# The recurrent mixer computed in two halves of its heads

## The chip, the cores and the metric

One core of a Trainium2 chip runs a whole forward pass of four layers in one launch. The metric is device time in microseconds (us), the median of several executions. A profiled execution of the same program gives the trace. Its engines are PE (TensorE, the matrix products), ACT (ScalarE), DVE (VectorE), POOL (GpSimd) and SP, the queue that issues the loads of the weights.

## What is computed

512 tokens of width 1024, everything in float32. The first block has a gMLP and convolution mixer, experts, a recurrent mixer, and experts again. The second block has two layers of attention with a gated feed-forward. The change lies in the recurrent mixer alone, cut here from the reference:

```python
def mixer_rglru(h, w_in, conv_w, conv_b, w_a, b_a, w_x, b_x, lam, w_out):
    gate, xr = jnp.split(h @ w_in, [D_RNN], axis=-1)          # 1024 -> 2 x 1024
    gate = jax.nn.gelu(gate)
    xr = causal_conv(xr, conv_w) + conv_b                     # 4 taps along the tokens
    xh = xr.reshape(bsz, t_len, LRU_HEADS, LRU_HEAD_DIM)      # 8 heads of 128
    r = sigmoid(einsum('bthi,hij->bthj', xh, w_a).reshape(...) + b_a)
    i = sigmoid(einsum('bthi,hij->bthj', xh, w_x).reshape(...) + b_x)
    log_a = (8.0 * r) * log_sigmoid(lam)
    a = exp(log_a)
    b = sqrt(-expm1(2.0 * log_a)) * (i * xr)
    _, hseq = associative_scan(combine, (a, b), axis=1)       # along the tokens, each channel by itself
    return (gate * hseq) @ w_out
```

No channel of it depends on another between the products with `w_in` and `w_out`, except within a head of 128 channels. So the eight heads can be worked in any order.

## The kernel before

Each engine has one program, a Python closure in `mixer_rglru`: `tensor`, `scalar`, `vector`, `gpsimd`. An engine works its instructions in the order in which they are written, and waits on counting semaphores (`x_conv`, `i_x`, `a_sq`, `q_done`, `b_root`, `scanned`, `y_mult`, `yhi`, `ylo`). Order and buffers are both fixed by hand.

**The products.** A float32 matrix is split into a high part (rounded to fp32r, by ACT in `W.hi`) and a low remainder (by DVE for even halves, by POOL for odd ones, in `W.lo`), and a product is three fp32r matmuls per tile: high by high, high by low, low by high. One 1024 x 512 piece of `w_in` is two units of 1 MB, so four halves, which are the four steps of a product of 96 matmuls. A raw unit sits in one of 4 raw slots and a split half in one of 6 split slots. Half s+6 is split when PE has used half s. SP issues the loads in the order of the plan (`plan_lru`), each when its raw slot was left: by the two low splits of the unit before it or, for the unsplit unit `gates`, by PE's last matmul with it. A load that waits holds all the later ones.

**The order on PE.** `xr 0` and `xr 1` (the two 512-column halves of the recurrent branch, heads 0 to 3 and 4 to 7), `gt 0` (first half of the gate branch), the gates (16 float32 matmuls, two for each head, line 1026, each of which shows as two in the trace), `gt 1`, then the product with `w_out` in two halves, `lruo 0` (line 605) and `lruo 1` (line 625). Step k of `lruo` waits for `ylo` k, the low part of feature block k of gate times state.

**The other engines.** ACT copies the results of `xr` out of PSUM (`bank_to`, line 680) and DVE convolves them with four taps (lines 1094 and 1097) into XC. After `gt 0` with its gelu, ACT takes the 16 sigmoids (line 680 with a bias from PK), POOL multiplies i by the convolved input (line 1134), and ACT takes exp, square and tanh for each head (lines 1051, 1057, 1058), DVE one combination (line 1106, `q_done`), then ACT eight square roots (line 1061), and DVE for each head a product and the scan (lines 1114, 1115). POOL multiplies heads 0 to 3 by the gate (line 1139), ACT rounds them to the high part (line 1064), DVE takes the low part (line 1110). Those four low parts stand on DVE's queue behind the sixth scan. Heads 4 to 7 get their product, high and low part after `gt 1` (lines 1124, 1074, 1110).

The square of a head lies in XT, a buffer of four heads that also holds what the convolution reads; so the squares of heads 4 to 7 wait for the combination of the head four before. AA (the decays) lies over XC, so exp of a head waits until POOL has read its convolved input.

The PSUM banks are eight, taken in turn; a product of 4 banks waits until the bank's last user has been read out.

Of the kernel before, what the change touches and what calls it, by code (L numbers as in the profile page):

```python
# [11 lines left out]
ALU = mybir.AluOpType  # L12
# [91 lines left out]
def up(signal, instruction):  # L104
    instruction.then_inc(signal.h, 1)
    signal.n += 1
    return signal.n
# [195 lines left out]
def program(nc, A, pack, const, out):  # L303
# [690 lines left out]

    def plan_lru():
        w = A["c_w_in"][0]
        for key, c0 in ((("xr", 0), 1024), (("xr", 1), 1536), (("gt", 0), 0)):
            plan_cols(key, w, c0, 512)
        W.add("gates", [(8, 128, A["c_w_a"][0].rearrange("h i j -> i h j")),
                        (8, 128, A["c_w_x"][0].rearrange("h i j -> i h j"))], split=False)  # L1000
        plan_cols(("gt", 1), w, 512, 512)
        plan_out("lruo", A["c_w_out"][0])

    def mixer_rglru(rows, late):
# [5 lines left out]
        AA = at(8192, 8, 512)  # L1010
        YH = at(8192, 8, 512, dt=F32R)
        YL = at(20480, 8, 512, dt=F32R)
        gates = W.of["gates"][0]
        H = rows.H

        def tensor():
            tensor_first_product(rows, ("xr", 0), 4, 512, ba, True)
            for key in (("xr", 1), ("gt", 0)):
                tensor_product(key, ALL4, 512, H, ba, feature=True)
            PE.wait_dma(W.s_raw[gates.slot], gates.arrived)  # L1020
            wg = W.raw[gates.slot][:, :].rearrange("p (g h j) -> p g h j", g=2, h=8)
            for h in range(8):
                PE.wait_ge(x_conv, h + 1)
                for g in range(2):
                    bank = banks.take(ba)
                    n = up(ba.full, pe.matmul(bank[:, :], wg[:, g, h, :], XC[:, h, :], start=True, stop=True))
            W.raw_consumed_at[gates.n] = (ba.full, n)
            tensor_product(("gt", 1), ALL4, 512, H, ba, feature=True)
            tensor_out("lruo", (lambda k: YH[:, k, :], lambda k: YL[:, k, :]), lambda k: PE.wait_ge(ylo, k),
                       ahead=lambda: tensor_experts_turn(1, 0))  # L1030

        def scalar():
            scalar_rows(rows, None, late, False)
            scalar_log_sigmoid(SM[:, 40:48])
            for s in range(2):
                def taps_in(s=s):
                    for o in range(4):
                        bank = ba.next(S)
                        if s:
                            S.wait_ge(x_conv, o + 1)  # L1040
                        bank_to(XT[:, o, :], bank[:, :])
                scalar_product(("xr", s), taps_in)
            scalar_product(("gt", 0), scalar_banks(lambda o: GT[0][:, o, :], func=ACT.Gelu_apprx_tanh))
            for h in range(8):
                for dst, bias in ((RB, "c_b_a"), (IB, "c_b_x")):
                    bank = ba.next(S)
                    bank_to(dst[:, h, :], bank[:, :], ACT.Sigmoid, bias=col(bias, h))
            S.wait_ge(lam_ready, 1)
            for h in range(8):
                S.wait_ge(i_x, h + 1)  # L1050
                up(a_exp, act.activation(AA[:, h, :], RB[:, h, :], ACT.Exp, scale=SM[:, 32 + h:33 + h]))
                S.wait_ge(a_exp, h + 1)
                if h < 4:
                    S.wait_ge(x_conv, 4 + h + 1)
                else:
                    S.wait_ge(q_done, h - 3)
                up(ss, act.activation(XT[:, h % 4, :], AA[:, h, :], ACT.Square))
                up(a_sq, act.activation(RB[:, h, :], RB[:, h, :], ACT.Tanh, scale=SM[:, 80 + h:81 + h]))
            for h in range(8):
                S.wait_ge(q_done, h + 1)  # L1060
                up(b_root, act.activation(RB[:, h, :], RB[:, h, :], ACT.Sqrt))
            for m in range(4):
                S.wait_ge(y_mult, m + 1)
                up(yhi, act.activation(YH[:, m, :], GT[0][:, m, :], ACT.Copy))

            def gelu_1():
                for o in range(4):
                    bank = ba.next(S)
                    S.wait_ge(q_done, 5 + o)
                    bank_to(GT[1][:, o, :], bank[:, :], ACT.Gelu_apprx_tanh)  # L1070
            scalar_product(("gt", 1), gelu_1)
            for m in range(4, 8):
                S.wait_ge(y_mult, m + 1)
                up(yhi, act.activation(YH[:, m, :], GT[1][:, m - 4, :], ACT.Copy))
            scalar_product(("lruo", 0))
            S.wait_ge(y_mult, 8)
            S.wait_ge(ylo, 8)
            load_moe(1)
            sqrt_table()
            return scalar_last_product(("lruo", 1), TAIL, lambda: scalar_experts_turn(1, 0))  # L1080

        def vector():
            vector_rows(rows, None, late, False)
            log_sigmoid_in(cols("c_lambda", 0, 8), SM[:, 40:48])
            log_sigmoid(SM[:, 32:40], cols("c_lambda", 0, 8), SM[:, 40:48], SM[:, 48:56], SM[:, 56:64])
            vstep(dve.tensor_scalar(SM[:, 32:40], SM[:, 32:40], 8.0, None, ALU.mult))
            up(lam_ready, dve.tensor_scalar(SM[:, 80:88], SM[:, 32:40], -1.0, None, ALU.mult))
            for s in range(2):
                def taps(s=s):
                    for o in range(4):  # L1090
                        m = 4 * s + o
                        y, g = XC[:, m, :], XT[:, o, :]
                        V.wait_ge(ba.free, m + 1)
                        vstep(dve.tensor_scalar(y, g, col("c_conv_w", 24 + m), col("c_conv_b", m), ALU.mult, ALU.add))
                        for j in (2, 1, 0):
                            d = 3 - j
                            ins = dve.scalar_tensor_tensor(y[:, d:T], g[:, 0:T - d], col("c_conv_w", 8 * j + m),
                                                           y[:, d:T], ALU.mult, ALU.add)
                            if j:
                                vstep(ins)  # L1100
                        up(x_conv, ins)
                vector_product(("xr", s), taps)
            vector_product(("gt", 0))
            for h in range(8):
                V.wait_ge(a_sq, h + 1)
                up(q_done, dve.scalar_tensor_tensor(RB[:, h, :], XT[:, h % 4, :], 1.0, RB[:, h, :], ALU.add, ALU.mult))

            def low(m):
                V.wait_ge(yhi, m + 1)
                up(ylo, dve.tensor_tensor(YL[:, m, :], GT[m // 4][:, m % 4, :], f32(YH[:, m, :]), ALU.subtract))  # L1110
            for h in range(8):
                V.wait_ge(b_root, h + 1)
                V.wait_ge(i_x, h + 1)
                vstep(dve.tensor_tensor(IB[:, h, :], IB[:, h, :], RB[:, h, :], ALU.mult))
                up(scanned, dve.tensor_tensor_scan(RB[:, h, :], AA[:, h, :], IB[:, h, :], 0.0, ALU.mult, ALU.add))
                if h == 5:
                    for m in range(4):
                        low(m)
            vector_product(("gt", 1))
            for m in range(4, 8):  # L1120
                V.wait_ge(ba.free, 8 + 4 + 16 + m - 3)
                V.wait_ge(scanned, m + 1)
                y = GT[1][:, m - 4, :]
                V.wait_total(y_mult, up(y_mult, dve.tensor_tensor(y, y, RB[:, m, :], ALU.mult)))
                low(m)
            return vector_out("lruo", norm_for_experts(1), lambda: vector_experts_turn(1, 0))

        def gpsimd():
            gpsimd_late(late)
            for key in (("xr", 0), ("xr", 1), ("gt", 0)):  # L1130
                gpsimd_product(key)
            for h in range(8):
                G.wait_ge(ba.free, 8 + 4 + 2 * h + 2)
                up(i_x, pool.tensor_tensor(IB[:, h, :], IB[:, h, :], XC[:, h, :], ALU.mult))
            for m in range(4):
                G.wait_ge(ba.free, 8 + m + 1)
                G.wait_ge(scanned, m + 1)
                y = GT[0][:, m, :]
                up(y_mult, pool.tensor_tensor(y, y, RB[:, m, :], ALU.mult))
            for key in (("gt", 1), ("lruo", 0), ("lruo", 1)):  # L1140
                gpsimd_product(key)
# [1407 lines left out]
```

## Time and profile before

| | us |
|---|---|
| median of 3 runs | 2706.59 |
| lowest and highest | 2702.04, 2707.36 |
| the profiled execution | 2703.67 |
| its span in the profile | 2702.3 |
| PE busy in it | 2592.2 |
| the recurrent mixer's products, first to last start | about 700 to 869 |

Times in a trace are counted from the start of the span. A timeline line shows when a group of like instructions began, its length, engine, line, operation and count, and in brackets how long the engine had been idle before it and what released it ("issue": nothing that the profile shows). Starts of two neighbouring groups give PE's pace best, since the ends of matmuls are modelled.

### The profile page before, as it was taken

What the parts mean: (1) busy time and instruction counts of PE and PEld (TensorE: products, weight loads), DVE (VectorE), ACT (ScalarE), POOL (GpSimd) and SP (SyncE); (2) the same over time, 40 slices, a digit from 0 to 9 for tenths busy, and PEclk for the clock granted to TensorE, in tenths of its full rate; (3) what the DMA queues carried; (4) which work ended last, traced back from release to release, by engine and by line L of the source; (5) the groups of instructions that cost most, each with busy time, mean ns of one, the idle gap of its engine ahead of it and who ended that gap; (6) DMA issues with size and microseconds to landing.
All of it is one profiled execution on the core that took longest, in us unless ns stands there. A gap on an engine that the chain in (4) does not pass through costs nothing.

```text
span 2702.3 us, 33251 instructions
## 1 busy us (share of the span) xinstructions
PE 2592.2 (96%) x13432; PEld 1818.3 (67%) x13432; DVE 1148.7 (43%) x2169; ACT 899.4 (33%) x1740; POOL 360.3 (13%) x165
## 2 busy tenths in 40 slices
PE   7998999999998899999979999999999999999999
PEld 6875444444766444444467778888888777888887
DVE  2543323332646332232256343562554534365254
ACT  3431111111464111111154554442345445443233
POOL 3200000000331000000021011222222001122222
PEclk9999999999898999999989999999999999999999
DMA  5229999999311999999932011223231201223212
GB/s 198 79 81 418 419 422 421 421 421 418 118 62 57 419 419 421 421 421 420 421 122 79 32 63 48 94 94 110 68 113 59 79 33 62 79 94 109 78 63 86
DMA packets 139003, 543.28 MB, mean 201 GB/s; under 512 B 18784, under 2 KB 30304, under 8 KB 89696
## 3 DMA queue, kind: packets, MB, share of 16 engines
q1 hardware_dynamic: 129232, 536.94, 50.8%
q10 hardware_dynamic: 9616, 4.18, 0.6%
q8 instruction: 109, 1.79, 0.3%
q14 instruction: 46, 0.38, 0.0%
HBM read 538.99 MB, written 2.10 MB: 200 GB/s over the span
## 4 chain that ended last, share of the span: by engine, by line
PE 90%; DVE 5%; ACT 2%; issue 2%; DMA 0%; POOL 0%; SPq 0%; DVEq 0%; ACTq 0%
PE ps L603 23%; PE ps L1363 16%; PE ps L605 14%; PE ps L1385 8%; PE ps L1338 5%; PE ps L625 4%; PE ps L537 4%; PE ps L1398 3%; PE ps L1939 2%; PE ps L1399 2%; PE ps L1912 2%; PE ps L1931 1%; PE ps L538 1%; PE ps L455 1%; DVE w L278 1%
## 5 line engine op out<-in xcount | busy, mean ns | idle before, releaser
L603 PE MATMUL ps<-w,w 128*128 128x512 f32 x2976 | 679.9, 390 | 2.6 <-POOL w L278 2.6
L603 PEld LDWEIGHTS ps<-w,w 128*128 128x128 f32 x2976 | 559.0, 188 | 119.7 <-POOL w L278 3.4
L278 POOL TENSOR_TENSOR w<-w,w 128x1024 fp32r<-128x1024 f32 (+2 forms) x139 | 337.2, 2435 | 2182.9 <-ACT w L270 2182.9
L1363 PE MATMUL ps<-w,w 128*64 128x512 f32 x2048 | 451.6, 594 | 1.8 <-issue 1.8
L605 PE MATMUL ps<-w,w 128*128 128x512 f32 (+1 forms) x1872 | 410.9, 381 | 18.2 <-issue 15.2
L270 ACT ACTIVATE w<-w 128x1024 fp32r<-128x1024 f32 (+2 forms) x260 | 252.7, 1001 | 436.2 <-PE ps L603 196.9
L605 PEld LDWEIGHTS ps<-w,w 128*128 128x128 f32 x1872 | 339.9, 189 | 85.5 <-issue 19.7
L278 DVE TENSOR_TENSOR w<-w,w 128x1024 fp32r<-128x1024 f32 (+2 forms) x121 | 200.7, 1666 | 386.8 <-ACT w L270 384.4
L1363 PEld LDWEIGHTS ps<-w,w 128*64 128x64 f32 x2048 | 146.0, 137 | 285.6 <-issue 285.6
L1615 DVE TENSOR_TENSOR X<-ps,X 128x512 f32<-128x512 f32 x256 | 163.0, 682 | 163.0 <-PE ps L1399 161.9
L1385 PE MATMUL ps<-w,w 128*64 128x512 f32 x1024 | 226.8, 595 | 0.8 <-ACT w L1449 0.8
L1385 PEld LDWEIGHTS ps<-w,w 128*64 128x64 f32 x1024 | 70.6, 137 | 139.8 <-issue 138.9
L2345 DVE SCALAR_TENSOR_TENSOR w<-ps,PK,w 128x511 f32<-128x511 f32 (+1 forms) x176 | 131.8, 749 | 75.8 <-ACT w L2301 72.6
L1338 PE MATMUL ps<-w,w 128*128 128x256 f32 x1024 | 131.3, 288 | 4.9 <-DVE w L1586 4.9
L1338 PEld LDWEIGHTS ps<-w,w 128*128 128x128 f32 x1024 | 130.2, 196 | 7.6 <-DVE w L1586 5.1
L1603 DVE TENSOR_TENSOR w<-ps,w 128x512 f32<-128x512 f32 x32 | 34.8, 1086 | 212.1 <-PE ps L1363 212.1
L625 PE MATMUL ps<-w,w 128*128 128x512 f32 x528 | 122.1, 390 | 0.9 <-DVE X L703 0.9
L1398 PE MATMUL ps<-w,w 128*128 128x512 f32 x256 | 111.8, 437 | 4.6 <-DVE w L1622 4.6
L625 PEld LDWEIGHTS ps<-w,w 128*128 128x128 f32 x528 | 98.7, 188 | 21.5 <-issue 1.3
L1622 DVE SCALAR_TENSOR_TENSOR w<-ps,w,w 128x512 fp32r<-128x512 f32 x64 | 45.1, 747 | 159.1 <-ACT w L1494 159.1
L1494 ACT ACTIVATE w<-ps,w 128x512 fp32r<-128x512 f32 x64 | 40.5, 684 | 204.0 <-PE ps L1385 204.0
L537 PE MATMUL ps<-w,w 128*128 128x256 f32 x768 | 99.9, 294 | 8.3 <-POOL w L278 6.7
(251 smaller groups left out, 2325.3 us busy)
## 6 DMA issues: line engine op xcount, KB each, us to landing
w<-in_moe_w_gate SPq DMA_DIRECT2D x128, 1024.0 KB, 14.0
w<-in_moe_w_up SPq DMA_DIRECT2D x128, 1024.0 KB, 16.4
w<-in_moe_w_down SPq DMA_DIRECT2D x128, 1024.0 KB, 13.0
w<-in_w_up SPq DMA_DIRECT2D x40, 1024.0 KB, 5.1
w<-in_w_down SPq DMA_DIRECT2D x20, 1024.0 KB, 5.1
w<-in_w_in SPq DMA_DIRECT2D x16, 1024.0 KB, 5.1
w<-in_ab_w_in SPq DMA_DIRECT2D x10, 1024.0 KB, 5.1
w<-in_c_w_in SPq DMA_DIRECT2D x8, 1024.0 KB, 5.1
```

What stands on the lines that cost most here:

```text
L270: up(self.whi, self.S.e.activation(hi, raw, ACT.Copy))
L278: up(self.wlo[self.low[s][0]], lane.e.tensor_tensor(lo, raw, hi.bitcast(F32), ALU.subtract))
L537: return pe.matmul(bs[o][:, t], w[:, P * o:P * o + P], a(k)[:, t], start=first, stop=stop)
L603: ins = pe.matmul(bank[:, :], wp[:, k, P * o:P * o + P], ap(k0 + k), start=first, stop=stop)
L605: ins = pe.matmul(bank[:, 0:width], ap(k0 + k)[:, P * o:P * o + P], wp[:, k, :], start=first, stop=stop)
L625: ins = pe.matmul(bank_of(o)[:, 0:width], ap(k)[:, P * o:P * o + P], wp, start=(k == 0 and pi == 0), stop=(hi is rows[-1][0] and pi == 2))
L1338: i = pe.matmul(bank[:, 256 * k:256 * k + 256], HB[part][:, c, t:t + P], SELR[:, c, :], start=(part == 0 and c == 0), stop=(part == 1 and ...
L1363: ins = pe.matmul(bank[64 * e:64 * e + 64, :], XG[p % 3][:, 4 * u + k, 64 * e:64 * e + 64], w[e][:, k, :], start=(u == 0 and k == 0), stop ...
L1385: ins = pe.matmul(two[n][64 * e:64 * e + 64, :], HDT[:, 2 * u + k, 64 * e:64 * e + 64], w[e][:, k, 512 * n:512 * n + 512], start=(u == 0 a ...
L1398: pe.matmul(bank[:, :], s_, YH[:, 512 * n:512 * n + 512], start=True, stop=False)
L1615: up(bx.free, dve.tensor_tensor(x, bank[:, :], x, ALU.add))
L2345: ins = dve.scalar_tensor_tensor(y[:, d:T], bank[:, 0:T - d], col("conv_w_2", 132 * i + 44 * tap + f), y[:, d:T], ALU.mult, ALU.add)
```

## The change

The heads are worked in two groups, 0 to 3 and 4 to 7, and every engine's program follows. PE's order becomes `xr 0`, `xr 1`, gates of heads 0 to 3, `gt 0`, gates of heads 4 to 7, `gt 1`, `lruo`. The gates' weights become two unsplit units. ACT's chain (sigmoids, exp, square, tanh, then roots) runs once for each group; the squares of heads 0 to 3 go to the buffer of `gt 0`. The roots and scans of the first group are put into the work for `gt 0`, behind its first split. The splits of the first two halves of `gt 1`, which stood in the work for `xr 1`, are put behind the first group's chain (`behind_gates`). The low parts of heads 0 to 3 follow all the scans.

```diff
     def plan_lru():
         w = A["c_w_in"][0]
-        for key, c0 in ((("xr", 0), 1024), (("xr", 1), 1536), (("gt", 0), 0)):
-            plan_cols(key, w, c0, 512)
-        W.add("gates", [(8, 128, A["c_w_a"][0].rearrange("h i j -> i h j")),
-                        (8, 128, A["c_w_x"][0].rearrange("h i j -> i h j"))], split=False)
-        plan_cols(("gt", 1), w, 512, 512)
+        for s in range(2):
+            plan_cols(("xr", s), w, 1024 + 512 * s, 512)
+        for s in range(2):
+            W.add("gates", [(4, 128, A[name][0][4 * s:4 * s + 4].rearrange("h i j -> i h j")) for name in ("c_w_a", "c_w_x")],
+                  split=False)
+            plan_cols(("gt", s), w, 512 * s, 512)
...
+        HEADS = (range(0, 4), range(4, 8))
+        behind_gates = late_halves(("xr", 1), 2)
+        def squared(h):
+            return GT[0][:, h, :] if h < 4 else XT[:, h - 4, :]
         def tensor():
...
+            tensor_product(("xr", 1), ALL4, 512, H, ba, feature=True)
+            for s in range(2):
+                gates = W.of["gates"][s]
+                wg = W.need_raw(gates, PE)[:, 0:1024].rearrange("p (g h j) -> p g h j", g=2, h=4)
+                for h in HEADS[s]:
+                    PE.wait_ge(x_conv, h + 1)
+                    for g in range(2):
+                        bank = banks.take(ba)
+                        n = up(ba.full, pe.matmul(bank[:, :], wg[:, g, h % 4, :], XC[:, h, :], start=True, stop=True))
+                W.raw_consumed_at[gates.n] = (ba.full, n)
+                tensor_product(("gt", s), ALL4, 512, H, ba, feature=True)
...
         def scalar():
...
-                scalar_product(("xr", s), taps_in)
+                scalar_product(("xr", s), taps_in, tail=2 * s)
+            def decays(hs):
+                for h in hs:
+                    for dst, bias in ((RB, "c_b_a"), (IB, "c_b_x")):
+                        bank = ba.next(S)
+                        bank_to(dst[:, h, :], bank[:, :], ACT.Sigmoid, bias=col(bias, h))
+                S.wait_ge(lam_ready, 1)
+                for h in hs:
+                    S.wait_ge(i_x, h + 1)
+                    up(a_exp, act.activation(AA[:, h, :], RB[:, h, :], ACT.Exp, scale=SM[:, 32 + h:33 + h]))
+                    S.wait_ge(a_exp, h + 1)
+                    if h > 3:
+                        S.wait_ge(x_conv, h + 1)
+                    up(ss, act.activation(squared(h), AA[:, h, :], ACT.Square))
+                    up(a_sq, act.activation(RB[:, h, :], RB[:, h, :], ACT.Tanh, scale=SM[:, 80 + h:81 + h]))
+            def roots(hs):
+                for h in hs:
+                    S.wait_ge(q_done, h + 1)
+                    up(b_root, act.activation(RB[:, h, :], RB[:, h, :], ACT.Sqrt))
+            def gelu_0():
+                for o in range(4):
                     bank = ba.next(S)
+                    S.wait_ge(q_done, 1 + o)
+                    bank_to(GT[0][:, o, :], bank[:, :], ACT.Gelu_apprx_tanh)
+            decays(HEADS[0])
+            for h in behind_gates:
+                W.hi(h)
+            scalar_product(("gt", 0), gelu_0, second=lambda: roots(HEADS[0]))
+            decays(HEADS[1])
+            roots(HEADS[1])
...
         def vector():
...
+                vector_product(("xr", s), taps, tail=2 * s)
...
-                if h == 5:
-                    for m in range(4):
-                        low(m)
+            factors(HEADS[0])
+            for h in behind_gates:
+                W.lo(h, V)
+            vector_product(("gt", 0), second=lambda: scans(HEADS[0]))
+            factors(HEADS[1])
+            scans(HEADS[1])
+            for m in range(4):
+                low(m)
             vector_product(("gt", 1))
...
         def gpsimd():
             gpsimd_late(late)
+            for s in range(2):
+                gpsimd_product(("xr", s), tail=2 * s)
+            def inputs(hs):
+                for h in hs:
+                    G.wait_ge(ba.free, 8 + 4 * (h // 4) + 2 * h + 2)
+                    up(i_x, pool.tensor_tensor(IB[:, h, :], IB[:, h, :], XC[:, h, :], ALU.mult))
+            inputs(HEADS[0])
+            for h in behind_gates:
+                W.lo(h, G)
+            gpsimd_product(("gt", 0))
+            inputs(HEADS[1])
             for m in range(4):
-                G.wait_ge(ba.free, 8 + m + 1)
+                G.wait_ge(ba.free, 8 + 8 + m + 1)
                 G.wait_ge(scanned, m + 1)
```

`factors` is the combination of line 1106 for a group of heads, and `scans` the product and scan of lines 1114 and 1115.

## Rows read from the trace of the kernel before

**Rows 1.** The page: engines' busy time and share of the span.
```profile
PE 2592.2 (96%) x13432; PEld 1818.3 (67%) x13432; DVE 1148.7 (43%) x2169; ACT 899.4 (33%) x1740; POOL 360.3 (13%) x165
```

**Rows 2.** PE's waits over the span: total, times, longest.
```profile
PE ps L605 <- issue: 15.2, 1, 15.2
```

**Rows 3.** PE's timeline, from xr 1 to lruo 1.
```profile
726.63 43.71 PE L603 MATMUL ps<-w,w 128*128 128x512 f32 x192
770.18 13.89 PE L1026 MATMUL ps<-w,w 128*128 128x512 f32 x32
783.51 22.34 PE L603 MATMUL ps<-w,w 128*128 128x512 f32 x96
821.04 24.87 PE L605 MATMUL ps<-w,w 128*128 128x512 f32 x96 [15.19 <-issue]
845.75 4.47 PE L625 MATMUL ps<-w,w 128*128 128x512 f32 x19
```

**Rows 4.** Windows: length; busy PE, PEld, DVE, ACT, POOL; granted clock; DMA.
```profile
820.00:825.00 5.00, 3.96 (x9) 3.14 (x10) 4.97 (x6) 3.13 (x6) 2.17 (x2) 0.50 0.01 3
```

**Rows 5.** ACT's timeline, from gt 0's read-out to the splits before lruo.
```profile
768.33 2.64 ACT L680 ACTIVATE w<-ps 128x512 f32<-128x512 f32 x4 [0.98 <-PE ps L603]
773.23 5.56 ACT L680 ACTIVATE w<-ps,PK 128x512 f32<-128x512 f32 x9
...
784.81 1.28 ACT L1051 ACT_TABLE_LOAD   x1
786.11 0.72 ACT L1051 ACTIVATE w<-w,SM 128x512 f32<-128x512 f32 x1
...
793.69 0.71 ACT L1051 ACTIVATE w<-w,SM 128x512 f32<-128x512 f32 x1
...
801.36 1.28 ACT L1061 ACT_TABLE_LOAD   x1
802.66 4.28 ACT L1061 ACTIVATE w<-w 128x512 f32<-128x512 f32 x8
...
815.89 2.93 ACT L270 ACTIVATE w<-w 128x1024 fp32r<-128x1024 f32 x3
```

**Rows 6.** DVE's timeline: end of the convolution, first scans, low parts, heads 4 to 7.
```profile
760.47 1.22 DVE L278 TENSOR_TENSOR w<-w,w 128x1024 fp32r<-128x1024 f32 x1
...
803.32 0.69 DVE L1114 TENSOR_TENSOR w<-w,w 128x512 f32<-128x512 f32 x1 [1.25 <-ACT w L1061]
...
805.19 0.67 DVE L1114 TENSOR_TENSOR w<-w,w 128x512 f32<-128x512 f32 x1
...
818.17 4.57 DVE L1110 TENSOR_TENSOR w<-w,w 128x512 fp32r<-128x512 f32 x4
...
830.68 0.69 DVE L1124 TENSOR_TENSOR w<-w,w 128x512 f32<-128x512 f32 x1
...
832.74 0.69 DVE L1124 TENSOR_TENSOR w<-w,w 128x512 f32<-128x512 f32 x1
```

**Rows 7.** Line 1110 by itself: duration in ns, least, median, most.
```profile
L1110 DVE TENSOR_TENSOR w<-w,w x8: 677/692/2767, 818.2 to 838.3; 128x512 fp32r<-128x512 f32 x8
```

**Rows 8.** POOL's timeline: inputs of four heads, and the split beside line 1110.
```profile
774.57 4.94 POOL L1134 TENSOR_TENSOR w<-w,w 128x512 f32<-128x512 f32 x4 [0.23 <-ACT w L680]
...
817.96 2.43 POOL L278 TENSOR_TENSOR w<-w,w 128x1024 fp32r<-128x1024 f32 x1 [2.63 <-ACT w L270]
```

**Rows 9.** PE's timeline elsewhere: a short idle time and what ran after it.
```profile
1977.79 8.50 PE L603 MATMUL ps<-w,w 128*128 128x512 f32 x36 [1.28 <-POOL w L278]
```

**Rows 10.** SP's waits from 600 to 900 us.
```profile
SPq L254 <- PE ps L625: 83.9, 1, 83.9
```

**Rows 11.** SP's timeline: the first load for the experts of the second layer.
```profile
869.47 2.06 SPq L254 DMA_DIRECT2D w<-in_moe_w_gate  x4
```

**Rows 12.** DMA issues by source from 650 to 870 us: count, size, us to landing.
```profile
w<-in_c_w_in SPq DMA_DIRECT2D x8, 1024.0 KB, 5.1
```

More of the change, by code:

```diff
@@ L1012, in mixer_rglru @@
         YL = at(20480, 8, 512, dt=F32R)
-        gates = W.of["gates"][0]
         H = rows.H
+        HEADS = (range(0, 4), range(4, 8))
+        behind_gates = late_halves(("xr", 1), 2)
+        def squared(h):
+            return GT[0][:, h, :] if h < 4 else XT[:, h - 4, :]
         def tensor():
             tensor_first_product(rows, ("xr", 0), 4, 512, ba, True)
[L1018 to L1028, printed above, removed]
+            tensor_product(("xr", 1), ALL4, 512, H, ba, feature=True)
[9 more added lines that the diff above has]
+                tensor_product(("gt", s), ALL4, 512, H, ba, feature=True)
             tensor_out("lruo", (lambda k: YH[:, k, :], lambda k: YL[:, k, :]), lambda k: PE.wait_ge(ylo, k),
@@ L1041, in taps_in @@
                         bank_to(XT[:, o, :], bank[:, :])
-                scalar_product(("xr", s), taps_in)
-            scalar_product(("gt", 0), scalar_banks(lambda o: GT[0][:, o, :], func=ACT.Gelu_apprx_tanh))
-            for h in range(8):
-                for dst, bias in ((RB, "c_b_a"), (IB, "c_b_x")):
-                    bank = ba.next(S)
[L1047 to L1058, printed above, removed]
@@ L1059, in scalar @@
-            for h in range(8):
-                S.wait_ge(q_done, h + 1)
-                up(b_root, act.activation(RB[:, h, :], RB[:, h, :], ACT.Sqrt))
+                scalar_product(("xr", s), taps_in, tail=2 * s)
[13 more added lines that the diff above has]
+                    up(a_sq, act.activation(RB[:, h, :], RB[:, h, :], ACT.Tanh, scale=SM[:, 80 + h:81 + h]))
@@ L1101, in taps, with factors, scans @@
                         up(x_conv, ins)
[L1102 to L1106, printed above, removed]
+                vector_product(("xr", s), taps, tail=2 * s)
+            def factors(hs):
+                for h in hs:
+                    V.wait_ge(a_sq, h + 1)
+                    up(q_done, dve.scalar_tensor_tensor(RB[:, h, :], squared(h), 1.0, RB[:, h, :], ALU.add, ALU.mult))
+            def scans(hs):
+                for h in hs:
+                    V.wait_ge(b_root, h + 1)
+                    V.wait_ge(i_x, h + 1)
+                    vstep(dve.tensor_tensor(IB[:, h, :], IB[:, h, :], RB[:, h, :], ALU.mult))
+                    up(scanned, dve.tensor_tensor_scan(RB[:, h, :], AA[:, h, :], IB[:, h, :], 0.0, ALU.mult, ALU.add))
             def low(m):
@@ L1110, in low @@
                 up(ylo, dve.tensor_tensor(YL[:, m, :], GT[m // 4][:, m % 4, :], f32(YH[:, m, :]), ALU.subtract))
[L1111 to L1115, printed above, removed]
-                if h == 5:
-                    for m in range(4):
-                        low(m)
+            factors(HEADS[0])
[6 more added lines that the diff above has]
+                low(m)
             vector_product(("gt", 1))
@@ L1129, in gpsimd @@
             gpsimd_late(late)
[L1130 to L1134, printed above, removed]
+            for s in range(2):
+                gpsimd_product(("xr", s), tail=2 * s)
+            def inputs(hs):
+                for h in hs:
+                    G.wait_ge(ba.free, 8 + 4 * (h // 4) + 2 * h + 2)
[5 more added lines that the diff above has]
+            inputs(HEADS[1])
             for m in range(4):
-                G.wait_ge(ba.free, 8 + m + 1)
+                G.wait_ge(ba.free, 8 + 8 + m + 1)
                 G.wait_ge(scanned, m + 1)
```

## The prediction

> **What bounds the kernel now.** I read the page first: PE is busy 96% of the span [rows 1]. So only two things can shorten this kernel, less work on PE or less idle time of PE, and the change leaves PE's work as it is. The list of PE's waits comes next: one wait of 15.2 us stands before line 605, the first product with `w_out` [rows 2]. PE's timeline shows where it lies. `gt 1` starts at 783.51 and `lruo 0` only at 821.04 [rows 3]. A product of 96 matmuls takes 21.78 us from start to start: xr 1 and gt 0 are 192 matmuls and take 770.18 - 726.63 = 43.55 [rows 3]. So PE was through with `gt 1` at 783.51 + 21.78 = 805.3. `lruo 0` then takes 845.75 - 821.04 = 24.71, which is 2.93 more than 21.78, and the granted clock after the idle time is 0.50, the lower of the two levels, 1.2 GHz of 2.4 [rows 4]. In all the hole costs 821.04 - 805.29 + 2.93 = 18.7 us. That is the most the change can give, since the rest of the program is not touched.
>
> What fills the hole: `lruo 0` waits for the low part of head 0 (line 1110). It lies at the end of one chain through all eight heads, sigmoids, then exp, square and tanh (786.11 on), then roots (802.66 on) [rows 5], then scans (803.32 on), and then line 1110 at 818.17 behind the sixth scan [rows 6]. Its first instruction took 2.77 us where the median is 0.69 [rows 7], because POOL was splitting from 817.96 for 2.43 us beside it [rows 8]: it ended at 820.94, and PE went on at 821.04.
>
> **The change, part by part.** PE's work is the same in another order. The gates take 783.51 - 770.18 = 13.33 us [rows 3], now twice 6.67. If nothing waits, `gt 1` starts at 783.5 as before, and the second gates, call their start G, at 776.84. The first gates start at 748.40, `gt 0` at 755.07. I follow the chain from G, with distances of before.
>
> The second group's chain:
> - The first sigmoid came 3.05 us after the first matmul of the gates (773.23 - 770.18), behind gelu, a split and a table load, which stand there again. Nine took 5.56, so eight take 4.94: G + 8.0. This also fits the pace of PE (sigmoids were through 1.3 after the gates, at 784.8, and 6.67 + 1.3 = 8.0) [rows 3, 5].
> - Table load: exp starts 1.30 after the last sigmoid [rows 5]: G + 9.3.
> - Four heads of exp, square and tanh: the fifth exp started at 793.69, 7.58 after the first [rows 5], and the last tanh runs some 0.1 on: G + 17.0.
> - Table load before the roots 1.30, first product 803.32 - 802.66 = 0.66 after the first root [rows 5, 6]: G + 18.95.
> - Four products with scans, undisturbed 805.19 - 803.32 = 1.87 each [rows 6]: G + 26.4.
> - Line 1110 for head 0: 0.69 alone, 2.77 beside a split of POOL [rows 7]: G + 27.1 or G + 29.2.
>
> PE asks for it at G + 6.67 + 21.78 = G + 28.45. So it waits between nothing and 0.8 us. I take the disturbed value: four roots (half of 4.28), four rounded parts of about 0.55 and two splits of 0.98 (three took 2.93) [rows 5] put POOL's split at about G + 18.3 + 2.1 + 2.2 + 2.0 = G + 24.7, in the last scan, and it must come before line 1110 or in the middle of the scans. The scans themselves used to lose about 1 us each to POOL's products of line 1139; those products now come long before.
>
> The first group's chain lies beside `gt 0`. ACT: sigmoids through at 748.40 + 8.0 = 756.4 at the latest (PE's pace gives 756.0), exp from 757.3, tanh to 765.0, the two postponed splits and one more of 0.98 to 768.0, table load to 769.3, four roots to 771.5, two splits to 773.5, table load to 774.8. It must then read out `gt 0`, whose first bank is full 1.85 before the end of the product (770.18 - 768.33 [rows 3, 5]), at 775.0. So the 21.8 us of `gt 0` hide it with only 0.2 us to spare. That is the thin place: what ACT loses here goes straight into G's chain, less some 0.6 us that a late read-out gets back by running at 0.52 instead of at PE's pace. I add 0.3 us. DVE: the convolution ended at 760.47, and four inputs of POOL, 4.94 us in all [rows 8], can at most stand in its way for their own length, so 765.4; the roots need the combinations only from 769.3. DVE's next work for PE is the combination for G's group, so the first scans have some 15 us to spare. POOL has those 4.94 us and three splits of 2.43 [rows 8] in 25 us.
>
> Three table loads more, 1.3 us each, are all in these sums: the first group's sigmoid, exp and root loads lie beside `gt 0`. Costs of DVE's and POOL's moved instructions are nothing as long as PE has work; without `gt 0` over them the first group would cost some 19 us.
>
> The loads. SP now holds the two units of `gt 1` and the first of `w_out` until the first gates are done, 755.1; a load of 1 MB lands 5.1 later [rows 12], 760.2, and ACT splits it at 765. The other three units of `w_out` wait for the second gates, 783.5, as they now wait for the gates; no split asks before 800. The gates' weights are two loads of half the size, the first ahead of `gt 0`, with over 30 us to spare. Nothing here costs.
>
> Behind the first part: heads 4 to 7. DVE has three more low parts and two splits, up to about G + 35.5 with one disturbance (2.4), and then 2.06 us for each head (832.74 - 830.68 [rows 6]): the low part of head 4 at about 814.7. PE asks for it four steps of 2.72 us after its start at 806, at 817. Margin 2.3, and growing by 0.66 with each head. No second wait.
>
> What is late next: the first low part again, by 0.8 + 0.3 = 1.1 us, 1.2 with the 0.1 from the semaphore to PE's start (820.94 to 821.04). Such an idle time does not lower the clock: elsewhere, after 1.28 us, 36 matmuls took 8.50 [rows 9], that is 0.24 each, against 21.78 / 96 = 0.23 here. If it did, it would cost up to the 2.9 us of now.
>
> **The sum.** 18.7 - 1.2 = 17.5 us. Against the profiled execution's 2703.67 that is 2686.2; against the median 2706.59 it is 2689.1. The three timed runs and the profiled one have a mean of 2704.9, which gives 2687.4. I forecast 2688.
>
> Does the gain reach the end? The loads of the next experts start at 869.47 [rows 11], released by the last matmul of `lruo 1`, for which SP had waited 83.9 us [rows 10]. They move with PE, and so does all behind them.
>
> **The rivals.**
> (a) ACT overruns `gt 0`. For it: 0.2 us of margin in a row of 26 us; exp waits for POOL's product and the root for DVE's combination, and both engines have more beside them in the new order than in the rows I took. Against: all durations are measured. An overrun of 3 to 4 us makes PE wait 4 to 5 us in all, and with that the clock falls as now (2.9): 18.7 - 4.5 - 2.9 = 11.3 us, so 2694 from the forecast's base.
> (b) A change of function costs ACT more than the load. In the rows it doesn't: exp starts at 786.11, 1.30 after the load began, the roots 1.30 after theirs [rows 5]. If each change cost 1.4 us more, four in the first group would overrun `gt 0` by 5.3 and three behind G would add 4.1: 18.7 - 1.2 - 9.4 - 2.9 = 5.2 us of gain, 2700. The Trainium skill's page "ScalarE: Activation LUTs", section "What ACT_TABLE_LOAD costs", says just this (1283 ns and a drain of about 1380 ns), and its section on table sets advises to batch calls by set, which this change undoes. The trace has the 1.28 us and no drain behind it.
> (c) Slower: the four-head chain waits for the convolution of heads 4 to 7. DVE works it (760.47 before) ahead of the first combinations, and the roots, the read-out of `gt 0` and so PE's second gates now stand behind those. From about 769 on, each us of delay is a us of PE's time. To be slower by 0.2% the convolution would have to end after 793. POOL's four small products cannot do that by themselves; it takes DVE and POOL blocking each other far longer than the 2.1 us of one meeting (2.77 less 0.69) [rows 7].
> (d) The gain is taken back behind the mixer, because the experts' stage has a pace of its own: about 2705. Against it stand the two rows of the loads [rows 10, 11].
>
> **Chances.** Forecast (PE waits up to 3 us) 0.77, (a) 0.13, (b) 0.03, (c) 0.03, (d) 0.04. The lowest of the runs less the whole hole is 2702.0 - 18.7 = 2683.3, and I take 2682.5 as the low end; the high end takes in (a): 2697. About 0.2% or 5.4 us is what a measurement of this kernel can tell from no change. Faster 0.93, same 0.04, slower 0.03.
>
> **What would show it.** In the profile after: no wait of 15 us before `lruo 0`, but one of 0 to 2 us, with the granted clock at 1.00 through `lruo 0`; two groups of 16 gate matmuls, the second starting 28.4 us after the first; line 1110's first low part 27 to 30 us after the second gates' start; ACT's read-out of `gt 0` within 0.5 us of PE's last steps of it; four sets of roots and exp loads where there were two. Wrong would be: a wait of PE at the second gates (case a or b), drains behind the table loads (b), the first combination after 769 (c), or an experts' stage longer than before (d).

## The result, and the profile after

The changed kernel takes 2688.18 us (median of 4 runs, 2686.67 to 2689.76) against 2706.07 (4 runs, 2702.04 to 2707.36): ratio 0.9936, 95% interval 0.9919 to 0.9954. A second measurement of both gave 0.9941 (0.9927 to 0.9954), 2689.88 against 2706.4. By the medians that is 16.5 to 17.9 us less; the two intervals allow 12 to 22 us and 12 to 20 us. The forecast was 2688, its sum 17.5 us. So the time shows the gain, and its exact size is read from the traces.

PE's timeline of the changed kernel, the stretch of [rows 3] (start, length, engine, line, operation, count, idle time before):

```profile
726.00 21.95 PE L603 MATMUL ps<-w,w 128*128 128x512 f32 x96
747.79 7.03 PE L1032 MATMUL ps<-w,w 128*128 128x512 f32 x16
754.25 22.34 PE L603 MATMUL ps<-w,w 128*128 128x512 f32 x96
776.43 7.03 PE L1032 MATMUL ps<-w,w 128*128 128x512 f32 x16
782.89 22.34 PE L603 MATMUL ps<-w,w 128*128 128x512 f32 x96
805.43 22.04 PE L605 MATMUL ps<-w,w 128*128 128x512 f32 x96 [0.20 <-issue]
827.31 16.49 PE L625 MATMUL ps<-w,w 128*128 128x512 f32 x72
```

Line 1032 holds the gates, now in two groups. The idle time before `lruo 0` is 0.20 us where it was 15.19. `lruo 0` takes 827.31 - 805.43 = 21.88 instead of 24.71. From the first matmul of `xr 1` to the first of `lruo 1` it is 101.31 us; before it was 845.75 - 726.63 = 119.12 [rows 3]. I use this stretch as the measure of all experiments: it holds the whole of what was changed, and 17.8 us were gained in it.

The window of [rows 4] had the lower level, 0.50, in `lruo 0`. Two windows in the changed kernel's `lruo 0`, at 1.00, as are all six from 800 to 830 (length, busy PE, PEld, DVE, ACT, POOL, granted clock, DMA):

```profile
810.00:815.00 5.00, 5.00 (x24) 4.14 (x23) 3.51 (x5) 1.26 (x2) 0.00 (x0) 1.00 0.00 0
820.00:825.00 5.00, 5.00 (x23) 4.14 (x23) 1.23 (x1) 2.45 (x4) 2.48 (x1) 1.00 0.77 157
```

ACT's first group beside `gt 0`, and the start of the second, answering [rows 5]:

```profile
749.90 3.07 ACT L680 ACTIVATE w<-ps,PK 128x512 f32<-128x512 f32 x5
...
755.57 1.28 ACT L1058 ACT_TABLE_LOAD   x1
756.86 0.72 ACT L1058 ACTIVATE w<-w,SM 128x512 f32<-128x512 f32 x1
...
764.45 2.94 ACT L270 ACTIVATE w<-w 128x1024 fp32r<-128x1024 f32 x3
767.40 1.28 ACT L1068 ACT_TABLE_LOAD   x1
768.70 2.20 ACT L1068 ACTIVATE w<-w 128x512 f32<-128x512 f32 x4
770.80 1.99 ACT L270 ACTIVATE w<-w 128x1024 fp32r<-128x1024 f32 x2
772.81 1.28 ACT L680 ACT_TABLE_LOAD   x1
774.59 2.64 ACT L680 ACTIVATE w<-ps 128x512 f32<-128x512 f32 x4 [0.49 <-PE ps L603]
...
779.48 4.74 ACT L680 ACTIVATE w<-ps,PK 128x512 f32<-128x512 f32 x8
784.24 1.28 ACT L1058 ACT_TABLE_LOAD   x1
785.54 0.72 ACT L1058 ACTIVATE w<-w,SM 128x512 f32<-128x512 f32 x1
```

From the table load before exp (755.57) to the end of the one for gelu (774.09) ACT works without a gap beside `gt 0`, and then waits 0.49 us for PE; the last three sigmoids before that still wait for PE's gates, 0.17 us each. No drain stands behind a table load: 755.57 + 1.28 = 756.85, and exp starts at 756.86.

DVE's end of the second group, answering [rows 6], and POOL's split beside it, answering [rows 8]:

```profile
795.19 0.69 DVE L1132 TENSOR_TENSOR w<-w,w 128x512 f32<-128x512 f32 x1 [0.80 <-ACT w L1068]
...
801.44 3.30 DVE L1133 TENSOR_TENSOR_SCAN w<-w,w 128x512 f32<-128x512 f32 x1
804.67 2.46 DVE L1137 TENSOR_TENSOR w<-w,w 128x512 fp32r<-128x512 f32 x4
...
811.53 0.68 DVE L1151 TENSOR_TENSOR w<-w,w 128x512 f32<-128x512 f32 x1
812.98 0.69 DVE L1137 TENSOR_TENSOR w<-w,w 128x512 fp32r<-128x512 f32 x1 [0.77 <-ACT w L1093]
```

```profile
800.78 2.89 POOL L278 TENSOR_TENSOR w<-w,w 128x1024 fp32r<-128x1024 f32 x1 [6.94 <-ACT w L270]
```

POOL's split met the fourth scan of the group, which took 3.30 us instead of 1.22, and the low part of head 0 began at 804.67. PE started at 805.43. The low part of head 4 was there at 812.98 + 0.69 = 813.7, PE asked for it near 816.3.

### The profile page after: what moved, and what is told of

It is laid out like the page before. It is cut to its first block, busy times and chain, and to the rows that moved or that the text cites. A ratio compares the mean times of both kernels' runs of the same rounds, so it can differ in the third digit from the quotient of the medians.

```text
span 2688.4 us, 33253 instructions
## 1 busy us (share of the span) xinstructions
PE 2591.1 (96%) x13432; PEld 1816.7 (68%) x13432; DVE 1156.9 (43%) x2169; ACT 903.1 (34%) x1743; POOL 362.9 (14%) x165
## 4 chain that ended last, share of the span: by engine, by line
PE 92%; DVE 4%; ACT 2%; issue 1%; DMA 0%; POOL 0%; SPq 0%; DVEq 0%; ACTq 0%
PE ps L603 24%; PE ps L1397 17%; PE ps L605 14%; PE ps L1419 8%; PE ps L1372 5%; PE ps L625 4%; PE ps L537 4%; PE ps L1432 3%; PE ps L1973 2%; PE ps L1433 2%; PE ps L1946 2%; PE ps L1965 1%; PE ps L538 1%; PE ps L455 1%; PE ps L1407 1%
## 6 DMA issues: line engine op xcount, KB each, us to landing
w<-in_moe_w_up SPq DMA_DIRECT2D x128, 1024.0 KB, 16.5
```

## The experiments

**What was to be told apart.** Theory: the hole was the length of one chain of work through eight heads on ACT and DVE, and it is closed because the first half of it now lies beside `gt 0`. Rivals: that it was only the place of four instructions on DVE's queue; that starting the chain a product earlier would do without two groups; that only ACT's part mattered. Then the margins: how thin the cover on ACT is, and whether a microsecond there reaches the end.

| kernel | idle before lruo 0 | stretch | median | ratio to before |
|---|---|---|---|---|
| before | 15.19 | 119.12 | 2706.07 | 1 |
| before, again | 15.21 | 119.02 | 2705.89 | 0.9999 (0.9990 to 1.0009) |
| changed | 0.20 | 101.31 | 2688.18 | 0.9936 (0.9919 to 0.9954) |
| changed, again | 0.21 | 101.29 | 2689.88 | 0.9941 (0.9927 to 0.9954) |
| low parts earlier, in the changed | 0 | 100.82 | 2691.78 | 0.9945 (0.9930 to 0.9960) |
| low parts one by one, in the before | 2.90 + 0.46 + 11.11 | 119.53 | 2706.05 | 1.0002 (0.9993 to 1.0012) |
| all gates first, one chain | 5.05, and 4.08 at the gates | 113.90 | 2700.84 | 0.9986 (0.9977 to 0.9995) |
| the same, split 16 amid the scans | 5.27, and 4.07 at the gates | 113.96 | 2700.80 | 0.9984 (0.9974 to 0.9993) |
| late scans | 12.21 | 115.98 | 2702.40 | 0.9987 (0.9977 to 0.9996) |
| 3 squares more, first group | 1.25 | 102.35 | 2690.08 | 0.9942 (0.9926 to 0.9959) |
| 3 squares more, second group | 2.30 | 103.41 | 2691.05 | 0.9941 (0.9925 to 0.9958) |
| 11 squares more, second group | 8.30 | 112.21 | 2699.14 | 0.9969 (0.9958 to 0.9979) |

Times in us. The stretch is from the first matmul of `xr 1` to the first of `lruo 1` in each kernel's trace. The ratio is to the kernel before as timed beside that kernel (its medians were 2706.0 to 2706.5), with its 95% interval.

**The kernels unchanged, once more.** No edit; both were run again for a second trace.

> The changed kernel once more, unchanged. If its gain is the closed hole before lruo 0 (15.2 us of idle time and 2.8 us at the lower clock), the ratio to the kernel before is 0.993 to 0.994, that is 17 to 19 us, and the trace again has no more than 0.5 us of PE's idle time before lruo 0. The profiled pair differed by only 13.9 us in span, because PE ran a few microseconds longer at the lower clock at three places after the mixer (near 857, 1626 and 2080 us). If that is chance, these places lie elsewhere or are gone in this trace; if the change causes them, they stand at the same instructions.

> The kernel before once more, unchanged, for a second trace of it. The idle time of 15.2 us before lruo 0 and the lower clock behind it stand again. If the stretches at the lower clock outside the mixer are chance, they lie at other places than in the first trace (near 20, 205, 695, 885, 1380, 1445 and 2265 us) or differ in length by 1 us or more; if they belong to the kernel, they are the same.

The stretch repeats within 0.1 us in both kernels. The rest of the program doesn't, in either kernel: behind the first matmul of `lruo 1` the spans have 2702.3 - 845.75 = 1856.6 and 1860.3 us before, 1861.1 and 1863.7 after. In the kernel before, the stretches at the lower clock stood at the same places again (near 20, 205, 695, 885, 1380, 1445 and 2265 us), some of them with other lengths, and one more near 2125. More on this in the last section.

**Low parts one by one, in the kernel before.** Does the queue's order alone make the hole?

```diff
-                if h == 5:
-                    for m in range(4):
-                        low(m)
+                if 1 <= h <= 4:
+                    low(h - 1)
```

> The kernel before with one edit: each of the four low parts of heads 0 to 3 stands behind the scan of the next head instead of all four behind the sixth. Rival theory (the hole is only the place of the low parts on DVE's queue): lruo 0 starts near 809 instead of 821 us and 12 to 14 us are gained, most of what the change gave. Chain theory (DVE is busy from the first scan at 803.3 to the product of head 4 at 830.7, whatever the order): lruo 0 starts near 809, but PE then waits at its fifth step for head 4, whose low part still comes near 832.8; lruo 1 starts at 832.8 + 4 x 2.72 = 843.7 instead of 845.75, so 2 us are gained, 5 at most.

PE's timeline:

```profile
807.19 10.11 PE L605 MATMUL ps<-w,w 128*128 128x512 f32 x36 [2.90 <-issue]
817.76 3.02 PE L605 MATMUL ps<-w,w 128*128 128x512 f32 x12 [0.46 <-DVE w L1110]
831.88 12.88 PE L605 MATMUL ps<-w,w 128*128 128x512 f32 x48 [11.11 <-DVE w L1110]
844.60 16.49 PE L625 MATMUL ps<-w,w 128*128 128x512 f32 x72
```

PE starts `lruo 0` 12 us earlier in the stretch (807.19 - 725.07 = 82.1 against 94.4 from `xr 1`), does half of it (48 matmuls), and waits 11.11 us for head 4. The whole gain turned into a new wait, down to nothing (119.53 against 119.12; I had expected 2 us of gain). The first rival falls. DVE is full from the first scan to the product of head 4, so the order inside it only chooses where PE waits. Its busy time between the two is 27.55 of 27.82 us (PE, PEld, then DVE):

```profile
801.77:829.59 27.82, 15.65 (x60) 11.66 (x58) 27.55 (x22) 13.26 (x20) 11.61 (x6) 0.86 0.00 1
```

**Late scans, in the changed kernel.** Does it need DVE's half of the chain to be split too?

```diff
-            vector_product(("gt", 0), second=lambda: scans(HEADS[0]))
+            vector_product(("gt", 0))
             factors(HEADS[1])
-            scans(HEADS[1])
+            scans(range(8))
```

> The changed kernel with the first group's four scans moved behind the roots of the second group, so that DVE works eight scans in a row again; PE's order and ACT's work stay. Chain theory: the scans begin near 795.2 us and, with POOL's products between them, take 14.9 us for six as in the kernel before and 3.7 for two more, with 2 us for a split of POOL: the first low part comes near 816.6 and PE, which asks near 805.1, waits 11 us and loses up to 2.9 us to the clock: 12 to 14 us over the changed kernel. If only ACT's functions filled the hole, the time stays within 3 us of the changed kernel.

PE and then the scans on DVE:

```profile
817.23 24.70 PE L605 MATMUL ps<-w,w 128*128 128x512 f32 x96 [12.21 <-issue]
```

```profile
794.35 1.23 DVE L1133 TENSOR_TENSOR_SCAN w<-w,w 128x512 f32<-128x512 f32 x1
...
796.19 2.20 DVE L1133 TENSOR_TENSOR_SCAN w<-w,w 128x512 f32<-128x512 f32 x1
...
814.36 4.57 DVE L1137 TENSOR_TENSOR w<-w,w 128x512 fp32r<-128x512 f32 x4
```

ACT's functions are split as in the changed kernel, and yet 14.7 of the 17.8 us are gone: 12.0 us more of idle time, and 24.54 instead of 21.88 for `lruo 0`. Four of the eight scans take about 2.20 us in place of 1.23, those that POOL's products with the gate run beside, as in the kernel before. So the rival that only ACT's part mattered falls: with ACT's part split alone, and PE's new order, 3.1 us of the 17.8 are gained. What the first group's scans cost behind `gt 0` is their own time (four times 1.87) and these meetings with POOL.

**All gates first, one chain.** Is it enough to begin a product earlier?

```diff
                 W.raw_consumed_at[gates.n] = (ba.full, n)
+            for s in range(2):
                 tensor_product(("gt", s), ALL4, 512, H, ba, feature=True)
...
-            decays(HEADS[0])
-            for h in behind_gates:
-                W.hi(h)
-            scalar_product(("gt", 0), gelu_0, second=lambda: roots(HEADS[0]))
-            decays(HEADS[1])
-            roots(HEADS[1])
+            decays(range(8))
+            scalar_product(("gt", 0), gelu_0, second=lambda: roots(range(8)))
...
-            factors(HEADS[0])
             for h in behind_gates:
                 W.lo(h, V)
-            vector_product(("gt", 0), second=lambda: scans(HEADS[0]))
-            factors(HEADS[1])
-            scans(HEADS[1])
+            factors(range(8))
+            vector_product(("gt", 0), second=lambda: scans(range(8)))
```

POOL's inputs follow in the same way, and the splits of `gt 1`'s first halves stand between the sigmoids and exp.

> The changed kernel with PE's order xr 0, xr 1, all sixteen gate matmuls, gt 0, gt 1, and one chain through all eight heads as in the kernel before, only begun a product earlier. If the early start of the chain closes the hole: PE waits only for the convolution of heads 6 and 7 (ready at 758.7 and 761.5 us in the changed kernel's trace, asked for at 757.6 and 760.4 and later), 2 to 3 us in all, no hole before lruo 0, and the time is 2 to 3 us over the changed kernel, 2690 to 2692. If the two groups are what closes it (one chain of eight heads is too long even beside two products), a hole of 5 us or more stands before lruo 0 and the time is 2698 or more.

```profile
747.25 10.46 PE L1032 MATMUL ps<-w,w 128*128 128x512 f32 x24
759.12 1.98 PE L1032 MATMUL ps<-w,w 128*128 128x512 f32 x4 [1.41 <-DVE w L1115]
763.77 3.07 PE L1032 MATMUL ps<-w,w 128*128 128x512 f32 x4 [2.67 <-DVE w L1115]
765.85 45.10 PE L603 MATMUL ps<-w,w 128*128 128x512 f32 x192
816.00 23.52 PE L605 MATMUL ps<-w,w 128*128 128x512 f32 x96 [5.05 <-DVE w L278]
```

It gains 5.2 us of the 17.8. PE waits twice: 4.08 us at the gates of the last two heads, since their convolution isn't through, and 5.05 before `lruo 0`. Those are 8.9 of the 12.6 us that it is slower than the changed kernel; `lruo 0` itself takes 23.36 instead of 21.88 us, and the rest, some 2 us, lies in the gates and `gt 0` (the window 765 to 770 has a granted clock of 0.71). With that the second reading of the expectation holds. The split of half 16 (halves are counted from `xr 0`; this is the first of `w_out`) stood last on DVE before the low parts, so I tried its place too:

```diff
-            vector_product(("gt", 0), second=lambda: scans(range(8)))
+            vector_product(("gt", 0), lambda: scans(range(4, 8)), second=lambda: scans(range(4)))
```

> The kernel with all gates ahead of gt 0, but with DVE's split of half 16 put between the fourth and the fifth scan instead of behind the eighth. PE waited 5.05 us before lruo 0 for that split and for the low part behind it. If the place of that split was the cause, the wait goes to 0 to 2 us and the time falls by 3 to 5 us. If the eight scans in a row with POOL's work beside them are, the wait falls by the split's 1.2 to 2 us only, to 3 to 4 us, and the time by 1 to 2 us.

The wait is 5.27 us, not smaller at all, and neither of the two forecasts came (0 to 2, 3 to 4). Before, DVE's split met one of POOL's and took 3.31 us:

```profile
811.99 3.31 DVE L278 TENSOR_TENSOR w<-w,w 128x1024 fp32r<-128x1024 f32 x1
```

With it out of the way the low parts meet POOL's splits, and the four take 6.75 us instead of 4.66; the longest single one takes 2.85.

```profile
814.36 6.75 DVE L1136 TENSOR_TENSOR w<-w,w 128x512 fp32r<-128x512 f32 x4
```

So one chain of eight heads begun earlier is still too long by 5 us beside two products, in both orders tried, and it asks for heads that the convolution hasn't reached. The early start is worth 5.2 us; the other 12.6 came only with the two groups. Other places of POOL's and DVE's splits in the single chain weren't tried.

**Low parts earlier, in the changed kernel.** The 0.20 us that are left.

```diff
                     up(scanned, dve.tensor_tensor_scan(...))
+                    if h == 5:
+                        for m in range(4):
+                            low(m)
...
             scans(HEADS[1])
-            for m in range(4):
-                low(m)
```

> The changed kernel with the four low parts of heads 0 to 3 put behind the second scan of the second group instead of the fourth. The chain theory says the first low part then comes at about 799.6 us instead of 805.4, and PE's rest of idle time (0.2 to 0.4 us) goes: 0.4 us at most, not measurable in the time. The rival, that the order of the low parts matters for PE by itself, would show 2 us or more.

The idle time is gone and the stretch is 0.5 us shorter (100.82), so the rival of 2 us or more falls. The time of the whole, 2691.78, can't be told from the changed kernel's 2689.88 in the same measurement, where single runs of either lie between 2687 and 2694. It is no better version.

**More work on ACT.** How thin is the cover, and does a microsecond reach the end? Squares whose result isn't used stand between the sigmoids and exp:

```diff
+                for _ in range(3 if hs[0] == 0 else 0):
+                    square(X[:, 0, 0:512], 512, SM[:, 12:13])
                 S.wait_ge(lam_ready, 1)
```

> The changed kernel with three more squares (512 columns, 0.82 us each, 2.45 in all) on ACT in the first group's chain; their result is not used. ACT has 0.49 us of idle time before gt 0's read-out and a late read-out saves 0.58 of PE's pace, so the second chain comes 1.4 us later and PE waits 1.6 us before lruo 0: 1.4 us over the changed kernel, or up to 4 if the clock falls. If the first group is hidden with several microseconds to spare: nothing.

> The changed kernel with the same three squares in the second group's chain: everything behind moves by 2.45 us and PE waits 2.6 to 2.8 us before lruo 0: 2.4 us over the changed kernel, 5 if the clock falls after such an idle time. If the chain has slack there: nothing.

> Eleven squares in the second group's chain, 9.0 us: PE waits 9.2 us before lruo 0 and the lower clock costs up to 2.9: 9 to 12 us over the changed kernel. The whole of it reaches the end if the stage of experts moves with the mixer's end; if that stage has a pace of its own, less.

The second and third differ in `hs[0] == 4` and 11. ACT's read-out of `gt 0` with three squares in the first group, and `lruo 0` with three in the second:

```profile
774.49 1.28 ACT L680 ACT_TABLE_LOAD   x1
775.79 2.06 ACT L680 ACTIVATE w<-ps 128x512 f32<-128x512 f32 x4
```

```profile
807.68 22.04 PE L605 MATMUL ps<-w,w 128*128 128x512 f32 x96 [2.30 <-issue]
```

The read-out no longer waits for PE and runs at 0.52 us a bank, 2.06 instead of 2.64. The three squares cost 2.1 us of ACT (0.7 each, as their full effect in the second group shows: 103.41 - 101.31 = 2.10; I had taken 0.82). Of these 2.1 the stretch lost 1.04 in the first group and all in the second. So the first group has 1.1 us of cover, 0.49 of idle time and 0.58 of slower read-out, and the second has none. In the time of the whole neither can be told from the changed kernel (ratios 0.9942 and 0.9941). Eleven squares make PE idle for 8.30 us and the stretch 10.9 longer: the 8.1 us that they add, and 24.68 instead of 21.88 for `lruo 0` at the lower clock:

```profile
812.66 24.84 PE L605 MATMUL ps<-w,w 128*128 128x512 f32 x96 [8.30 <-issue]
837.34 16.49 PE L625 MATMUL ps<-w,w 128*128 128x512 f32 x72
```

The medians follow: 2699.14 is 9 to 11 above the changed kernel, and by the ratios it is 8 to 9 (0.9969 against 0.9936 and 0.9941).

## Why the prediction was right

**The bound.** The hole was priced at 18.7 us. It was really 18.2: a product behind the gates takes 22.18 from start to start (754.25 to 776.43), not 21.78, and a group's eight gate matmuls take 6.46, not 6.67, so PE would have been free at 783.51 + 22.18 = 805.7 and the hole is 821.04 - 805.69, with 24.71 - 21.88 for the lower clock. Over PE's whole order the two errors cancel; in the hole they don't.

**The chain from G** (776.43 here). Step by step, predicted and measured distances: last sigmoid 8.0 and 7.8 (784.22); exp 9.3 and 9.1; first product of the scans 18.95 and 18.76; low part of head 0 finished 29.2 and 28.9 (805.36). Each of these is within 0.3 us. PE was free at 28.64 instead of 28.45 and started at 29.0, where the sum with its 1.2 us of waiting had it at 29.65. The meeting of POOL and DVE was forecast at G + 24.7 and came at 24.35 (800.78), and its price was that of [rows 7] once more: 3.30 - 1.22 = 2.1.

**The thin place on ACT** was named and sized: 0.2 us to spare predicted, 0.49 there. The 0.3 us that I added for it were not lost. That, and the bound, are why PE idled 0.20 us (0.36 from start to start) instead of 1.2: two errors of 0.8 in the wait and 0.5 in the hole, of opposite sign: 18.2 - 0.4 = 17.8 us where 18.7 - 1.2 = 17.5 was forecast. That the median then fell on 2688.18 is luck in its last two microseconds: the second measurement of the same kernel gave 2689.88, and the forecast took its base about 1 us below the median before.

**The second group of low parts**: 814.7 predicted, 813.7 measured, no wait. The loads cost nothing, as said.

**The rule of the Trainium skill** on table loads ("ScalarE: Activation LUTs", section "What ACT_TABLE_LOAD costs": a drain of 1380 ns at every change of set) gave rival (b) its 2700. This case's traces disagree: 1.29 and 1.30 us from the load's start to the next function, 755.57 to 756.86 and 784.24 to 785.54 above. By the same page's advice to batch calls by set (section "Table sets: the hidden batching unit") this change would be a bad one; here its three more loads lay under PE's product or inside the sum.

**The other rivals.** (a) did not come, but the squares show that it was 0.5 us of idle time away, 1.1 with the slower read-out. (c): the first combination of the first group stood behind the convolution until 761.53, where 769 would have begun to cost. The late scans show how meetings of DVE and POOL can add up to several us; here there was room. (d): SP's first load for the experts came at 851.03 instead of 869.47 [rows 11], 18.4 us earlier, and the eleven squares' 10.9 us in the stretch were 8 to 11 us at the end.

```profile
761.53 1.89 DVE L1126 SCALAR_TENSOR_TENSOR w<-w,w 128x512 f32<-128x512 f32 x3
```

```profile
851.03 2.08 SPq L254 DMA_DIRECT2D w<-in_moe_w_gate  x4
```

**What was wrong**: the sentence that an idle time of 1.28 us does not lower the clock. It rested on one row [rows 9]. In the changed kernel's trace, the same wait of 1.14 us before the same 48 matmuls near 1630 was followed by the full clock in one execution and by a slower stretch in another (next section). It had no price in the stretch itself, where even 2.30 us of idle time cost none. Nor did the sum have a term for the clock behind the mixer, where 1.6 and 1.4 us went at one place of the changed kernel's two traces (next section).

## What to carry to other kernels

When PE waits at the end of a chain, ask whether the chain is too long or only its order wrong: the low parts one by one moved the wait and gained nothing, while halving the chain and laying the first half beside a product gained nearly all of it (17.8 of 18.2 us). Write down the cover of the half that is hidden on each engine (here 1.1 us on ACT of 26); of what was put there later, all that exceeded this cover was paid, one for one. Split all engines' parts: with DVE's half left in one piece, 14.7 of 17.8 us came back.

## What the runs showed of the hardware

**The granted clock after the same idle time differs from one execution to the next.** The 48 matmuls of line 605 behind a wait of 1.14 us, in the kernel before (first line), the changed kernel, and the changed kernel again:

```profile
1642.32 11.13 PE L605 MATMUL ps<-w,w 128*128 128x512 f32 x48 [1.14 <-DVE w L523]
```

```profile
1625.43 12.74 PE L605 MATMUL ps<-w,w 128*128 128x512 f32 x48 [1.14 <-DVE w L523]
```

```profile
1632.69 11.16 PE L605 MATMUL ps<-w,w 128*128 128x512 f32 x48 [1.14 <-DVE w L523]
```

The window with the 12.74 had a mean granted clock of 0.66, so the lower of the two levels, 1.2 GHz, for a part of it:

```profile
1625.00:1630.00 5.00, 4.57 (x13) 3.69 (x14) 0.89 (x2) 0.93 (x1) 2.37 (x1) 0.66 0.08 11
```

Before `lruo 0`, even 2.30 us of idle time (three squares, second group) left it at 22.04 us, while 2.90 (low parts one by one) was followed by 36 matmuls in 10.11 us, where three eighths of 21.88 are 8.2. At the first place all twelve traces agree on two prices: 11.13 to 11.17 us in eight of them and 12.73 to 12.77 in four, one of these the kernel before with its low parts one by one. So there the price is nothing or 1.6 us, and it isn't the change that decides.

This is also why the first pair of profiled executions differs by 13.9 us in span and not by 17.8: behind the mixer the changed one was at the lower clock a little longer, for the most part at three places. One is the router's second product, 16 matmuls that took 1.95 us before:

```profile
859.32 3.33 PE L1340 MATMUL ps<-w,w 128*64 128x256 f32 x16 [1.68 <-DVE w L1274]
```

This line is of the changed kernel's second trace, and its first had the same stretch slow. The places near 1626 and 2080 us of the first trace are at full clock in the second, which has another near 1600. Does an earlier end of the mixer change how often this happens? The five traces without a hole (the changed kernel twice, low parts earlier, and both with three squares) have 1860 to 1867 us behind the first matmul of `lruo 1`, the two of the kernel before and its variant 1857 to 1860, and the four other variants, which have a hole, 1858 to 1864. At that product of the router the level goes with the kernel: it is slow (2.96 to 3.68 us) in the changed kernel twice, with low parts earlier and in both kernels with all gates first, and takes 1.95 in the other seven traces, the two of the kernel before among them. So 1.6 and 1.4 us of the gain were given back there in the two traces of the changed kernel, for a reason that no run isolates. The medians leave about 1 us for all of it (17.8 in the stretch, 16.5 to 17.9 in the time), their intervals more. For the rest of the program it stays open.

**An instruction of DVE that starts beside one of POOL can end a whole length of its own behind it.** In the changed kernel POOL's split ran from 800.78 to 803.67, and the scan begun at 801.44 ended at 804.74, 1.07 us later, where a scan alone takes 1.22. So scans took 2.20 us beside a POOL product and 3.30 beside a split, and a combination of 0.69 us took up to 1.71. I had expected this from [rows 7]; that the low parts can lose 4 us to it in a row (6.75 for four, against 2.46) I had not.
